# The first pass over eight experts: instructions written out in place of a loop on four engines

## The chip, the cores and the metric

The kernel runs on one core of a Trainium2 chip. The metric is the device time of one execution in microseconds. The kernel before takes 1589.56 us (median of three runs, 1588.62 to 1594.91).

## The reference

Two encoder layers on one sequence of 256 tokens of width 1024, all in float32. Layer 0 mixes tokens with dilated attention and a RWKV-7 scan and ends in a dense SwiGLU. Layer 1 mixes with a short convolution and a gated DeltaNet and ends in a mixture of experts, which is the part that matters here:

```python
def moe_swiglu(h, router, w_gate, w_up, w_down):
    probs = jax.nn.softmax((h @ router).astype(jnp.float32), axis=-1)
    top_p, top_i = lax.top_k(probs, TOP_K)                    # 2 of 8
    top_p = top_p / jnp.sum(top_p, axis=-1, keepdims=True)
    gates = einsum(top_p, one_hot(top_i, N_EXPERTS))
    out = jnp.zeros_like(h)
    for e in range(N_EXPERTS):                                # 8 experts, 1024 -> 3584 -> 1024
        out = out + gates[..., e:e+1] * swiglu(h, w_gate[e], w_up[e], w_down[e])
    return out
```

Each expert has three matrices of 1024 x 3584 floats. Every one of them is read once from HBM in a pass.

## The kernel before, in words

The five engines run five instruction streams, each written by hand in its own block and tied together by semaphores; no planner orders them. Up to the router (some 660 us) all streams are straight code. The expert stage follows.

A pass of the expert stage holds up to 96 tokens for every expert (three blocks of 32). If some expert was chosen by more than 96 tokens, a flag makes all engines run up to two further passes; otherwise the `If` at the end of each stream skips them. In a pass every expert is done in two halves of its 3584 hidden columns. A half, numbered n from 0 to 15, has three phases on TensorE: `project("gate")`, `project("up")` (both at line 3139, 192 matmul records) and `down` (line 3164, 336 records). That makes 48 phases. The function `phase` (line 569) gives their order: gate 0, up 0, gate 1, up 1, down 0, then gate n, up n, down n-1 for n from 2 on, and down 15 at the end.

Weights pass through one ring of eight units in SBUF, 896 KB each; one phase uses the whole ring. SyncE (`load_phase`, `load_unit`, line 618) waits for each unit until TensorE has released it in the phase before (`unit_ps`), then issues the DMA of the next phase's unit. TensorE waits for a unit's landing (`landed_e`) just before its first matmul on it. So a unit has one phase, less the time of its own use, to be issued, moved and landed.

ScalarE applies SiLU to the gate banks and scales an expert's result (`silu`, `result`). VectorE multiplies by the up banks and transposes (`hidden`), and computes the row numbers of the next expert's tokens. GpSimd gathers those rows from HBM and adds finished rows back by indirect DMAs; its stream has no loop in it.

Four streams write the middle of a pass as a hardware loop (`Fori`): SyncE with 7 turns of six phases (line 638), ScalarE with 6 turns (line 1297), VectorE with 6 turns (line 2188) and TensorE with 6 turns (line 3202). One TensorE turn is

```python
with pe.Fori(0, NE - 2) as i:
    project("gate", ps, i, 2); project("up", ps, i, 2); down(ps, i, 1)
    project("gate", ps, i, 3); next_rows(ps, i, 2)
    project("up", ps, i, 3);   turn_rows(ps, i, 2); down(ps, i, 2)
```

that is, phases 5 to 10 in the first turn, 11 to 16 in the second, and so on to phase 40. Before it phases 0 to 4 stand as straight code, behind it phases 41 to 47. Every semaphore target inside is an expression in i, such as `i * (6 * NU) + ...`, so in a loop it is a register's value, and the expert's number in a DMA source (`bass.ds(i + 1, 1)`) is one too.

Of the kernel before, what the change touches and what calls it, by code (L numbers as in the profile page):

```python
# [25 lines left out]
NE = 8  # L26
# [70 lines left out]
def hybrid_trunk(nc, A, out):  # L97
# [16 lines left out]
    with ctx:  # L114
# [446 lines left out]
        @block.sync  # L561
        def _(sp):
            def load(kind, n):
                s, prev, _ = where[kind, n]
                if prev:
                    sp.wait_ge(*used_up(*prev))
                v = ring[:, s * SLOT:(s + 1) * SLOT]
                v8 = v.rearrange("p (k n) -> p k n", k=KT)
                kt = "o (k p) n -> p (o k) n"
                if kind == "ev_in":  # L570
                    parts = [(v8, A["ev_w_in"][:, :, 512 * n:512 * n + 512].rearrange(kt, p=P))]
                elif kind == "lora1":
                    w = v[:, 0:KT * 384].rearrange("p (k n) -> p k n", k=KT)
                    parts = [(w[:, :, 64 * z:64 * z + 64], A["ev_w1"][:, z].rearrange(kt, p=P)) for z in range(2)]
                    parts += [(w[:, :, 128 + 64 * z:192 + 64 * z], A["ev_a1"][:, z].rearrange(kt, p=P)) for z in range(2)]
                    parts += [(w[:, :, 256:384], A["ev_g1"].rearrange(kt, p=P))]
                elif kind == "lora2":
                    parts = [(v[:, 0:512], A["ev_w2"].rearrange("o z r c -> (o z r) c")),
                             (v[:, 512:1024], A["ev_a2"].rearrange("o z r c -> (o z r) c")),
                             (v[:, 1024:1536], A["ev_g2"].rearrange("o r c -> (o r) c"))]  # L580
                elif kind in ("ev_out", "od_out"):
                    w = A["ev_w_out" if kind == "ev_out" else "od_w_out"]
                    parts = [(v8, w[:, :, 512 * n:512 * n + 512].rearrange(kt, p=P))]
                elif kind == "ffn_in":
                    parts = [(v8[:, :, 256 * i:256 * i + 256],
                              A[w][:, :, 256 * n:256 * n + 256].rearrange(kt, p=P))
                             for i, w in enumerate(("ev_ffn_gate", "ev_ffn_up"))]
                elif kind == "ffn_down":
                    k = min(4, FF // P - 4 * n)
                    parts = [(v[:, 0:k * D].rearrange("p (k n) -> p k n", k=k),  # L590
                              A["ev_ffn_down"][:, 512 * n:512 * n + k * P, :].rearrange(kt, p=P))]
                elif kind == "od_in":
                    parts = [(v8, A["od_w_in"][:, :, 512 * n:512 * n + 512].rearrange(kt, p=P))]
                for dst, src in parts:
                    if (kind, n) == ("ev_in", 0):
                        sp.dma_start(dst[:, 0:4, :], src[:, 0:4, :]).then_inc(w0_in, 16)
                        dst, src = dst[:, 4:8, :], src[:, 4:8, :]
                    sp.dma_start(dst, src).then_inc(landed[s], 16)

            for a in range(TT):  # L600
                sp.dma_start(x_sb[:, a, :], A["x"][0, P * a:P * a + P, :]).then_inc(x_in[a], 16)
            sp.dma_start(vecrows[0:N0, 0, :], A["vecs"][0:N0, :]).then_inc(vec_in, 16)
            sp.dma_start(vecrows[0:N1, 1, :], A["vecs"][N0:N0 + N1, :]).then_inc(vec_in, 16)
            load(*chunks[0][:2])
            load(*chunks[1][:2])
            sp.dma_start(pos_i[:, :], A["positions"].rearrange("b (a p) -> p (b a)", p=P),
                         allow_slow_non_contiguous=True).then_inc(small_in, 16)
            sp.dma_start(rows[:, :], A["rows"].to_broadcast([P, A["rows"].shape[1]])).then_inc(small_in, 16)
            sp.dma_start(wsmall[:, :], A["wsmall"]).then_inc(small_in, 16)
            for kind, n, _ in chunks[2:]:  # L610
                load(kind, n)
            if UPTO >= 4:
                packed_w = {"gate": A["od_moe_gate"], "up": A["od_moe_up"], "down": A["od_moe_down"]}

                def load_unit(kind, e, s, u):

                    src = packed_w[kind][e, NU * s + u].rearrange("o p n -> p (o n)")
                    sp.dma_start(ring[:, UNIT * u:UNIT * u + UNIT], src).then_inc(landed_e[u], 16)

                def load_phase(ps, i, kind, e, n):  # L620

                    f = phase(kind, n)
                    for u in range(NU):
                        if f or ps:
                            sp.wait_ge(unit_ps, units_used(ps, i, f - 1, u))
                        elif u < 7:
                            sp.wait_ge(*used_up(*before[-(-(UNIT * u + UNIT) // SLOT) - 1 if UNIT * u + UNIT <= NSTAT * SLOT
                                                       else NSTAT - 1]))
                        load_unit(kind, e, n % 2, u)

                def expert_pass(ps):

                    load_phase(ps, 0, "gate", slice(0, 1), 0)
                    load_phase(ps, 0, "up", slice(0, 1), 0)
                    load_phase(ps, 0, "gate", slice(0, 1), 1)
                    load_phase(ps, 0, "up", slice(0, 1), 1)
                    load_phase(ps, 0, "down", slice(0, 1), 0)
                    with sp.Fori(0, NE - 1) as i:
                        for n in (2, 3):
                            load_phase(ps, i, "gate", bass.ds(i + 1, 1), n)  # L640
                            load_phase(ps, i, "up", bass.ds(i + 1, 1), n)
                            load_phase(ps, i, "down", bass.ds(i + (n - 2), 1), n - 1)
                    load_phase(ps, 0, "down", slice(NE - 1, NE), 2 * NE - 1)

                def store(ps):

                    for q in range(4):
                        c = slice(512 * (q % 2), 512 * (q % 2) + 512)
                        sp.wait_ge(cmb_sb, 8 * ps + 2 * q + 2)
                        sp.dma_start(out[0, P * (q // 2):P * (q // 2) + P, c], x_sb[:, q // 2, c]).then_inc(stored, 16)  # L650

                expert_pass(0)
                store(0)
                sp.wait_ge(flag_rdy, 1)
                with sp.If(sp.value_load(flag[0:1, 0:1], min_val=0, max_val=1) > 0):
                    for ps in range(1, PASSES):
                        sp.wait_ge(stored, 64 * ps)
                        expert_pass(ps)
                        store(ps)
                    sp.wait_ge(stored, 64 * PASSES)  # L660
                sp.wait_ge(stored, 64)
# [149 lines left out]
        def _(act):  # L811
# [428 lines left out]
            if UPTO >= 4:  # L1240
# [52 lines left out]
                def all_experts(ps):  # L1293

                    silu(ps, 0, 0)
                    silu(ps, 0, 1)
                    with act.Fori(0, NE - 2) as i:
                        silu(ps, i, 2)
                        result(ps, i, 0)
                        silu(ps, i, 3)  # L1300
                    silu(ps, 0, 2 * NE - 2)
                    result(ps, 0, NE - 2)
                    silu(ps, 0, 2 * NE - 1)
# [15 lines left out]
        def _(dve):  # L1319
# [728 lines left out]
            if UPTO >= 4:  # L2048
# [128 lines left out]
                def all_experts(ps):  # L2177
# [7 lines left out]
                    next_rows(ps, 0, 1)  # L2185
                    hidden(ps, 0, 1)
                    weigh_tokens(ps, 0, 1)
                    with dve.Fori(0, NE - 2) as i:
                        select(bass.ds(i + 2, 1))
                        hidden(ps, i, 2)  # L2190
                        dve.wait_ge(rows_added, i * (16 * NB) + 16 * (ADDED * ps + TT + 1 + NB))
                        next_rows(ps, i, 2)
                        hidden(ps, i, 3)
                        weigh_tokens(ps, i, 2)
                    select_last(ps)
                    hidden(ps, 0, 2 * NE - 2)
                    hidden(ps, 0, 2 * NE - 1)
# [17 lines left out]
        def _(pe):  # L2215
# [855 lines left out]
            if UPTO >= 4:  # L3071
# [116 lines left out]
                def all_experts(ps):  # L3188
# [10 lines left out]
                    project("up", ps, 0, 1)  # L3199
                    turn_rows(ps, 0, 1)  # L3200
                    down(ps, 0, 0)
                    with pe.Fori(0, NE - 2) as i:
                        project("gate", ps, i, 2)
                        project("up", ps, i, 2)
                        down(ps, i, 1)
                        project("gate", ps, i, 3)
                        next_rows(ps, i, 2)
                        project("up", ps, i, 3)
                        turn_rows(ps, i, 2)
                        down(ps, i, 2)  # L3210
                    last_n = 2 * NE - 2
                    project("gate", ps, 0, last_n)
                    project("up", ps, 0, last_n)
# [53 lines left out]
```

## Time and profile before

| | us |
|---|---|
| median of three runs | 1589.56 |
| the profiled execution | 1595.33 |
| its span, first to last instruction | 1593.6 |
| expert stage, first matmul of phase 0 to the last of phase 47 | 659.96 to 1583.19 |
| mean granted clock of TensorE (1.00 is 2.4 GHz) | 0.98 |

The engine rows of a profile count an instruction as busy from its start to its end, and matmuls overlap, so a busy TensorE need not be at its peak. The chain of waits is followed backwards from the last instruction; "issue" in it is time in which an engine waited for nothing that the profile shows. The column PEclk is the clock granted to TensorE as a share of 2.4 GHz, and the DMA share is the mean busy share of the 16 DMA engines; it can pass 1.00 a little where packets overlap.

### The profile page before, as it was taken

To read this page: it belongs to the slowest core of one execution; us is meant where nothing else is said; L and a number is where in the kernel's file an instruction comes from. 1 tells how busy PE (TensorE), PEld (TensorE's weight loads), DVE (VectorE), ACT (ScalarE), POOL (GpSimd) and SP (SyncE) were. 2 spreads that over 40 slices of the span, in tenths; PEclk is the share of its full clock that TensorE was granted. 3 is DMA by queue.
4 is the path that set the end of the run, shared out by engine and by line. 5 is a ranking of instruction groups with operands and counts; after the bars stand their busy time and mean duration, and the time that the engine had idled before them with its cause. 6 is when DMAs were issued, how large, how long until landed. Compare 5 with 4: busy or idle time off the path is not lost.

```text
span 1593.6 us, 35986 instructions
## 1 busy us (share of the span) xinstructions
PE 1547.3 (97%) x16151; PEld 942.2 (59%) x16151; DVE 491.4 (31%) x897; ACT 329.6 (21%) x560; POOL 104.0 (7%) x145
## 2 busy tenths in 40 slices
PE   9999999999999999999998998998998998999998
PEld 5868886999989976534343444444444444444435
DVE  5888465655456683311001001001001001001000
ACT  5455333543358432200000000000000000000000
POOL 3004000000000010010010010010010010010000
PEclk9999799999999999999999998999999999999999
DMA  7510013555553410899999998998998998999995
GB/s 259 149 46 26 1 54 106 185 186 197 173 185 107 149 63 1 305 419 417 418 405 372 392 395 357 377 397 361 387 399 354 388 402 352 390 401 419 405 407 240
DMA packets 111360, 440.09 MB, mean 276 GB/s; under 512 B 12330, under 2 KB 38846, under 8 KB 111198
## 3 DMA queue, kind: packets, MB, share of 16 engines
q1 hardware_dynamic: 106014, 427.90, 68.9%
q0 software_dynamic: 5184, 9.70, 2.2%
q8 instruction: 142, 2.33, 0.6%
q14 instruction: 20, 0.16, 0.0%
HBM read 430.62 MB, written 6.95 MB: 275 GB/s over the span
## 4 chain that ended last, share of the span: by engine, by line
PE 92%; DVE 4%; issue 2%; ACT 1%; DMA 0%; SPq 0%; DVEq 0%
PE bank L3139 37%; PE bank L3164 18%; PE bank L2297 5%; PE bank L2298 5%; PE bank L2296 5%; PE bank L3021 2%; PE bank L2263 2%; PE bank L2726 2%; PE bank L2316 1%; PE bank L2277 1%; PE bank L2393 1%; PE bank L2329 1%; ACT ehf L1207 1%; PE bank L2518 1%; PE bank L2610 1%
## 5 line engine op out<-in xcount | busy, mean ns | idle before, releaser
L3139 PE MATMUL bank<-ring,arena 128*32 128x448 f32 x6144 | 597.5, 546 | 29.1 <-issue 28.4
L3139 PEld LDWEIGHTS bank<-ring,arena 128*32 128x32 f32 x6144 | 216.7, 111 | 394.7 <-issue 393.1
L3164 PE MATMUL bank<-ring,arena 128*32 128x256 f32 x5376 | 295.0, 379 | 0.0
L3164 PEld LDWEIGHTS bank<-ring,arena 128*32 128x32 f32 x5376 | 177.5, 110 | 115.6 <-issue 4.6
L2161 DVE TENSOR_TENSOR arena<-bank,arena 128x448 f32<-128x448 f32 x48 | 28.7, 598 | 572.6 <-PE bank L3139 572.6
L1282 ACT ACTIVATE arena<-bank 128x448 f32<-128x448 f32 x48 | 26.1, 543 | 594.8 <-PE bank L3139 594.8
L2297 PE MATMUL bank<-ringr,split 128*128 128x256 f32 (+1 forms) x488 | 146.9, 301 | 0.0
L2296 PE MATMUL bank<-ehr_,split 128*128 128x256 f32 x400 | 113.3, 283 | 0.0
L2298 PE MATMUL bank<-ehr_,ringr 128*128 128x256 f32 x400 | 111.9, 280 | 0.0
L1772 DVE TENSOR_TENSOR ringr<-ring,split 128x2048 fp32r<-128x2048 f32 x33 | 75.5, 2291 | 72.8 <-ACT split L1090 72.8
L2297 PEld LDWEIGHTS bank<-ringr,split 128*128 128x128 f32 x488 | 91.7, 188 | 4.0 <-issue 0.2
L782 POOL DMA_INDIRECT xsum<-arena,row_now x21 | 33.4, 1590 | 664.8 <-ACT arena L1290 660.6
L1090 ACT ACTIVATE split<-ring 128x2048 fp32r<-128x2048 f32 x33 | 63.0, 1912 | 63.2 <-DMA ring<-in_ev_ffn_up 31.7
L2298 PEld LDWEIGHTS bank<-ehr_,ringr 128*128 128x128 f32 x400 | 76.0, 190 | 0.0
L2296 PEld LDWEIGHTS bank<-ehr_,split 128*128 128x128 f32 x400 | 75.1, 188 | 0.4 <-issue 0.2
L2141 DVE COPY row_now<-row_next 128x3 int32<-128x3 int32 x7 | 1.2, 169 | 223.9 <-PE bank L3104 223.9
L1290 ACT ACTIVATE arena<-bank,small 128x256 f32<-128x256 f32 x21 | 8.4, 471 | 246.5 <-PE bank L3164 246.5
L2296 PE MATMUL bank<-split 128*128 128x512 f32 (+1 forms) x120 | 43.7, 364 | 0.0
L2857 PE MATMUL bank<-scr,ring 128*128 128x256 f32 x160 | 38.3, 388 | 0.3 <-issue 0.3
L2298 PE MATMUL bank<-split 128*128 128x512 f32 x88 | 34.6, 393 | 0.0
L2298 PE MATMUL bank<-split,ringr 128*128 128x256 f32 x112 | 31.5, 282 | 0.0
L2163 DVE STREAM_TRANSPOSE arena<-arena 128x448 f32<-128x448 f32 x48 | 31.0, 645 | 1.7
(566 smaller groups left out, 1591.7 us busy)
## 6 DMA issues: line engine op xcount, KB each, us to landing
ring<-in_od_moe_gate SPq DMA_DIRECT2D x128, 896.0 KB, 8.0
ring<-in_od_moe_up SPq DMA_DIRECT2D x128, 896.0 KB, 9.0
ring<-in_od_moe_down SPq DMA_DIRECT2D x128, 896.0 KB, 10.0
ring<-in_od_w_in SPq DMA_DIRECT2D x7, 2048.0 KB, 7.7
ring<-in_ev_ffn_gate SPq DMA_DIRECT2D x11, 1024.0 KB, 5.5
ring<-in_ev_ffn_up SPq DMA_DIRECT2D x11, 1024.0 KB, 8.0
ring<-in_ev_w_in SPq DMA_DIRECT2D x5, 2048.0 KB, 9.0
ring<-in_ev_ffn_down SPq DMA_DIRECT2D x5, 2048.0 KB, 7.7
```

The source lines that it names most:

```text
L782: pool.indirect_dma_start(xsum, bass.IndirectOffsetOnAxis(row_now[:, b:b + 1], 0), ysb[:, b, :], None, compute_op=ADD).then_inc(rows_added ...
L1090: act.activation(homes[q % NHOME], ring[:, v], ACT.Copy).then_inc(pc_hi, 1)
L1772: dve.tensor_tensor(ringr[:, v], ring[:, v], homes[q % NHOME].bitcast(F32), SUB).then_inc(pc_lo, 1)
L2263: last = pe.matmul(B[bank][:, :], h[:, k, P * a:P * a + P], w8[:, k, :], start=(k == 0), stop=(k == KT - 1))
L2296: pe.matmul(o, sh, mh, start=start, stop=False, skip_group_check=True)
L2297: pe.matmul(o, sh, ml, start=False, stop=False, skip_group_check=True)
L2298: return pe.matmul(o, sl, mh, start=False, stop=stop, skip_group_check=True)
L2726: last = pe.matmul(B[2 * n + a][:, :], yT[:, k, P * a:P * a + P], w8[:, k, :], start=(k == 0), stop=(k == KT - 1))
L2857: last = pe.matmul(B[t % 2][:, SEQ * f:SEQ * f + SEQ], w8[:, k, c:c + P], hT[:, k, :], start=(k == 0), stop=(k == KT - 1))
L3021: last = pe.matmul(B[2 * n + a][:, :], yTo[:, k, P * a:P * a + P], w8[:, k, :], start=(k == 0), stop=(k == KT - 1))
L3139: last = pe.matmul(bank[BT * g:BT * g + BT, 0:FC], xg[:, k % 2, P * b + BT * (k // 2):P * b + BT * (k // 2) + BT], ring[:, UNIT * k + FC * ...
L3164: last = pe.matmul(B[6 + b // 2][BT * g:BT * g + BT, DC * (b % 2):DC * (b % 2) + DC], hdT[:, n % 2, b, BT * kk:BT * kk + BT], pieces_of(q) ...
```

## The change

On SyncE, ScalarE, VectorE and TensorE the loop's body becomes a function `expert(i)`. In the first pass (`ps == 0`) a Python loop calls it with i = 0, 1, 2, ..., so that the instructions of every turn stand one behind the other, with constants in place of register values. The further passes keep the hardware loop. TensorE's part, and SyncE's:

```diff
-                    with pe.Fori(0, NE - 2) as i:
+                    def expert(i):
                         project("gate", ps, i, 2)
                         project("up", ps, i, 2)
                         down(ps, i, 1)
...
+                    if ps == 0:
+                        for i in range(NE - 2):
+                            expert(i)
+                    else:
+                        with pe.Fori(0, NE - 2) as i:
+                            expert(i)
```

```diff
-                    with sp.Fori(0, NE - 1) as i:
+                    def expert(i):
                         for n in (2, 3):
                             load_phase(ps, i, "gate", bass.ds(i + 1, 1), n)
...
+                    if ps == 0:
+                        for i in range(NE - 1):
+                            expert(i)
+                    else:
+                        with sp.Fori(0, NE - 1) as i:
+                            expert(i)
```

ScalarE and VectorE have the same edit around their loops of NE - 2 turns. GpSimd's stream is as before. No operation, wait or buffer is added, removed or moved in order.

## Rows read from the trace of the kernel before

**Rows 1.** The page, part 4: the chain that ended last, by engine.

```profile
PE 92%; DVE 4%; issue 2%; ACT 1%; DMA 0%; SPq 0%; DVEq 0%
```

**Rows 2.** The page, part 2: granted TensorE clock in 40 slices of 39.84 us.

```profile
PEclk9999799999999999999999998999999999999999
```

**Rows 3.** Costliest groups by line: records; busy us, mean ns; idle before, releaser.

```profile
L3139 PE MATMUL bank<-ring,arena 128*32 128x448 f32 x6144 | 597.5, 546 | 29.1 <-issue 28.4 <-DVE arena L2152 0.7
L3164 PE MATMUL bank<-ring,arena 128*32 128x256 f32 x5376 | 295.0, 379 | 0.0
```

**Rows 4.** The chain in order of time, 752 to 995: start us, us, what.

```profile
752.76 36.08 PE bank L3139 x384
...
844.53 18.27 PE bank L3164 x336
862.80 5.14 issue
867.94 3.94 PE bank L3139 x17
871.88 1.51 issue
873.38 34.40 PE bank L3139 x364
...
982.12 3.94 issue
```

**Rows 5.** TensorE's waits, 863 to 1456: releaser, us, times, longest.

```profile
PE bank L3139 <- issue: 28.4, 10, 5.1
```

**Rows 6.** Stretches: length, busy us (records) per engine, clock, DMA share, GB/s.

```profile
752.57:862.80 110.23, 110.23 (x1454) 47.44 (x1446) 8.99 (x21) 4.46 (x9) 7.68 (x6) 1.00 1.02 413
862.80:982.12 119.32, 112.68 (x1450) 51.87 (x1450) 8.99 (x21) 4.46 (x9) 7.70 (x6) 0.97 0.98 386
1101.60:1219.50 117.90, 112.84 (x1451) 50.90 (x1450) 8.99 (x21) 4.46 (x9) 7.71 (x6) 0.97 0.97 382
1337.88:1456.09 118.21, 112.50 (x1454) 52.21 (x1458) 9.69 (x24) 4.46 (x9) 7.71 (x6) 0.99 0.97 381
1456.09:1566.30 110.21, 110.21 (x1466) 47.85 (x1462) 7.16 (x12) 5.33 (x11) 5.97 (x5) 1.00 1.02 409
...
879.50:982.12 102.62, 102.62 (x1373) 48.34 (x1365) 8.99 (x21) 4.46 (x9) 7.70 (x6) 1.00 1.01 400
```

**Rows 7.** The same view around one turn's end.

```profile
862.00:868.00 6.00, 0.86 (x20) 0.29 (x16) 0.00 (x0) 0.00 (x0) 0.00 (x0) 0.77 1.01 413
868.00:874.00 6.00, 4.49 (x25) 1.19 (x29) 0.00 (x0) 0.00 (x0) 0.00 (x0) 0.66 0.60 245
```

**Rows 8.** Ring loads, to landing, at 700:753, 753:863, 880:982, 1456:1566 in that order.

```profile
DMA to landing us min/median/max: 10.5/13.4/14.5
DMA to landing us min/median/max: 10.5/12.2/14.1
DMA to landing us min/median/max: 6.0/7.5/10.8
DMA to landing us min/median/max: 7.0/8.7/12.1
```

**Rows 9.** DMA of 752.57 to 862.80: all packets; queue, packets, MB, share.

```profile
DMA packets 7585, 45.56 MB, mean 413 GB/s; under 512 B 875, under 2 KB 1259, under 8 KB 7570
q8 instruction: 12, 0.20, 0.7%
```

**Rows 10.** The same queue of 862.80 to 982.12.

```profile
q8 instruction: 14, 0.23, 0.7%
```

**Rows 11.** Waits of ScalarE and VectorE in the expert stage.

```profile
ACT arena L1282 <- PE bank L3139: 594.8, 48, 63.2
DVE arena L2161 <- PE bank L3139: 572.6, 16, 59.5
```

**Rows 12.** SyncE's queue in order of time, 835 to 880.

```profile
847.49 15.84 SPq L618 DMA_DIRECT2D ring<-in_od_moe_gate  x8
```

More of the change, by code:

```diff
@@ L1296, in all_experts @@
                     silu(ps, 0, 1)
-                    with act.Fori(0, NE - 2) as i:
+                    def expert(i):
                         silu(ps, i, 2)
@@ L1300, in all_experts @@
                         silu(ps, i, 3)
+                    if ps == 0:
+                        for i in range(NE - 2):
+                            expert(i)
+                    else:
+                        with act.Fori(0, NE - 2) as i:
+                            expert(i)
                     silu(ps, 0, 2 * NE - 2)
@@ L2187, in all_experts, with expert @@
                     weigh_tokens(ps, 0, 1)
-                    with dve.Fori(0, NE - 2) as i:
+                    def expert(i):
                         select(bass.ds(i + 2, 1))
@@ L2194, in all_experts @@
                         weigh_tokens(ps, i, 2)
+                    if ps == 0:
+                        for i in range(NE - 2):
+                            expert(i)
+                    else:
+                        with dve.Fori(0, NE - 2) as i:
+                            expert(i)
                     select_last(ps)
@@ L3201, in all_experts, with expert @@
                     down(ps, 0, 0)
-                    with pe.Fori(0, NE - 2) as i:
+                    def expert(i):
                         project("gate", ps, i, 2)
@@ L3210, in all_experts @@
                         down(ps, i, 2)
+                    if ps == 0:
+                        for i in range(NE - 2):
+                            expert(i)
+                    else:
+                        with pe.Fori(0, NE - 2) as i:
+                            expert(i)
                     last_n = 2 * NE - 2
```

## The prediction

> **What bounds the kernel now.** I read the chain that ended last first: TensorE holds 92% of it, and 2% is "issue", time that nothing in the profile explains [rows 1]. The grouped lines put that time in one place: the expert projections of line 3139 have 28.4 us of it in front of them, the down projections of line 3164 none [rows 3]. The record counts also say that only the first pass runs: 6144 is 32 projections of 192, and 5376 is 16 downs of 336. The further passes, which keep their loop, are skipped, so the edit covers all that is executed.
>
> Then the chain in order of time, to see where the 28.4 us stand. From 752.76 to 862.80, the loop's first turn, matmuls follow each other without a hole. Then come 5.14 us of nothing, 17 matmuls in 3.94 us, 1.51 us of nothing, and full pace again; at 982.12 it starts over [rows 4]. There are ten such holes in five pairs [rows 5], one pair for each of the loop's five jumps back. None stands at the entry of the loop (752.57) or at its exit (1456.09). I conclude that the cost is the jump: behind a taken branch TensorE has no instructions. The hole is not a semaphore, for it has no releaser and its place is the first instructions of the body.
>
> The third view prices a whole turn. The first turn, entered from above, takes 110.23 us; the second 119.32, the fourth 117.90, the last 118.21; the straight code behind the loop, with nearly the same work in it, 110.21 [rows 6]. The holes are only part of the 8 to 9 us: in the stretches around one the granted clock is 0.77 and 0.66 in place of 1.00 [rows 7], a mixture of 2.4 and 1.2 GHz, after TensorE had stood still. The clock by slices of 40 us almost hides that: it has one 8 in the whole expert stage [rows 2], so a short fall has to be looked for at the hole itself. Hence 17 matmuls in 3.94 us, 232 ns each, where 384 in 36.08 us are 94 ns each [rows 4].
>
> **The change, part by part.** *TensorE's jumps.* Five turns run from 862.80 to 1456.09, which is 593.29 us; five turns at the first one's 110.23 us are 551.15. The difference is 42.1 us: 28.4 holes [rows 5] and 13.7 slow clock behind them. Written out, each turn is entered as the first one was, from the instruction above it. I take all 42.1 away. A larger gain I exclude: the first turn already had the loop's register arithmetic in it and went at the pace of straight code, so that constants in place of registers save nothing on the path.
>
> *Instructions fetched.* The instruction queue brought 12 packets, 0.20 MB, in the first turn and 14, 0.23 MB, in the second [rows 9, 10]. So a turn is fetched anew each time in the loop too, and written out it is fetched no more often. Price: nothing, and a gain of at most 0.03 MB a turn. Its cover is that fetching runs ahead in straight code; what it would cost without that is the third rival.
>
> *The other three engines.* ScalarE and VectorE waited 594.8 and 572.6 us for TensorE's projections [rows 11]; their jumps lie in such waits, gone or not. SyncE's turn ends before phase 11's first load, which was issued at 847.49 [rows 12]. TensorE could release that unit after 48 of the 336 records of phase 10, that is at 844.53 + 48/336 x 18.27 = 847.1 [rows 4]: no delay from SyncE's jump is seen. All three: nothing. If one did show through, it would be a gain of at most a hole such as TensorE's, 5 us, five or six times over, but no wait of TensorE for them stands in the trace.
>
> *What is late next: the weights.* This is the only cost I can see. The 5 us at each jump also gave the DMAs time; the share fell to 0.60 behind the hole [rows 7]. Without it they must keep TensorE's pace from start to end. The room: a phase lasts 18.1 us and uses a unit for an eighth, 2.3, so that a load has 15.9 us from release to need. After a jump loads take 7.5 us (at most 10.8). Where no jump comes for long, they take 13.4 (14.5) before the loop, 12.2 (14.1) in the first turn, and 8.7 (12.1) behind the loop [rows 8]. So the queue grows by about 1 us a turn where it is short and shrinks by 1 where it is long. I expect it to settle near 12, under 15.9, as in the first turn, which ran with no wait for a landing at 413 GB/s. Bounds: nothing (the first turn), and, if 400 GB/s, the lowest rate of a stretch of 100 us at full share [rows 6], were all the DMAs can do: 45.56 MB [rows 9] then take 113.9 us a turn, 3.7 more, over 6.15 turns' worth to the end 22.6 us. I take 1.5 us, near the first turn, which is the nearest row: the same work, the same full queue.
>
> Sum for the profiled execution: 1595.33 - 42.1 + 1.5 = 1554.7 us. The median of the runs is 5.8 us lower. If those 5.8 us lie outside the jumps, the median becomes 1589.56 - 40.6 = 1549.0; if they lie in jumps that cost less in the other runs, it stays at 1554.7. The turns themselves differ by 1.4 us [rows 6], so part of it may. I take 1551.
>
> **Two rules against it.** The trace's jump costs 42.1/5 = 8.4 us. The Trainium skill (Advanced Engine Details and Errata, Control Flow Timing) gives about 51 ns for a branch and 108 for a compare-and-branch; an estimate by it is 5 x 0.16 = 0.8 us for all five, and the sum would be 1589. The holes disagree, unless they have another cause; that is the second rival. The trace moves 413 GB/s in the first turn. The Trainium skill (DMA: Bandwidth & Descriptors, Where 436 GB/s comes from) holds that some 358 GB/s bind a transfer from HBM to SBUF; an estimate by it is 45.56 MB in 127 us a turn, more than today's 118, and no gain at all. The trace, with 413, contradicts it here.
>
> **The rivals.**
> 1. *The DMAs take half back.* The queue keeps growing by 1 us a turn past 15.9, and TensorE waits in small pieces inside a phase, at the 400 GB/s bound: 1589.56 - 42.1 + 22.6 = 1570; the stretch between my forecast and there is this case's. For it: DMA share 1.01 to 1.02 wherever no jump is near. Against it: the shrinking queue of the first turn.
> 2. *The hole is not the jump's.* The body's head waits for something that the profile doesn't record, or the DMAs need the pause: the time stays 1589. For it: "issue" is only the absence of a recorded releaser. Against it: the first turn has the same head and no hole.
> 3. *Slower: straight code starves TensorE of instructions.* The place is the down phases, which use instructions fastest: 672 records (matmuls and their weight loads) in 18.27 us, so a packet of 16 KB, 256 instructions (0.23 MB in 14 packets), lasts 7.0 us. A packet fetched at a jump took up to 5.14 us. With loads that take 12.2 in place of 7.5 us a fetch could take 5.14 x 12.2/7.5 = 8.4 us and be 1.4 late. There are some 2.6 packets in each of 13 downs left after phase 10, 34 in all: 47 us lost, 5 more than is won, about 1595. It is slower from 8.2 us a fetch on. Against it: phases 7 and 10 ran with a long queue and no hole.
>
> **How the numbers follow.** Forecast, 1544 to 1557: 0.80. Rival 1, 1557 to 1575: 0.13. Rival 2, within 0.5% (8 us, about what a measurement here can tell from no change): 0.04. Rival 3: 0.03. So faster 0.93, same 0.04, slower 0.03. The range reaches from a little under the full 42.1 us off the fastest run, 1544, to the 400 GB/s bound, 1570.
>
> **What would show it.** Right: no "issue" in front of line 3139 after phase 10, a clock of 1.00 through the expert stage, turns of 110 to 111 us, loads that take 11 to 14 us, the span near 1553. Wrong in the DMA step: waits of TensorE for landings in short pieces, most in the phases in which rows are gathered and added back, and turns of 112 to 114. Wrong in the main step: holes at the same places, at 862.80 and then every 118 us, or new ones in the down phases.

## The result, and the profile after

The changed kernel takes 1542.72 us (median of four runs, 1540.90 to 1543.81) beside 1592.24 us for the kernel before (four runs, 1588.62 to 1602.31). The ratio is 0.968, 95% interval 0.963 to 0.973. It is faster, as forecast, but by 49.5 us where 40.6 were summed up, and 1.3 us below the forecast range. A second comparison, with six runs of it and eleven of the kernel before, gave 0.972 (0.967 to 0.977).

The page of the changed kernel: the chain by engine, the clock by slices, and the two groups that answer to [rows 1 to 3].

```profile
PEclk9999999999999999999999999999999999999999
...
PE 93%; DVE 4%; ACT 1%; issue 1%; DMA 0%; SPq 0%; DVEq 0%
...
L3160 PE MATMUL bank<-ring,arena 128*32 128x448 f32 x6144 | 581.7, 539 | 0.7 <-DVE arena L2166 0.7
...
L3185 PE MATMUL bank<-ring,arena 128*32 128x256 f32 x5376 | 293.0, 379 | 0.0
```

The 28.4 us of "issue" in front of the projections are gone, and so is the slow clock behind them: a projection's mean is 539 ns, where it was 546. The chain of the changed kernel in order of time answers to [rows 4]; the first line is the start of the expert stage:

```profile
648.96 18.25 PE bank L3160 x192
...
741.75 36.08 PE bank L3160 x384
...
833.52 18.27 PE bank L3185 x336
851.79 36.08 PE bank L3160 x384
...
943.56 18.27 PE bank L3185 x336
```

Down 10 (833.52) runs straight into gate 11 (851.79), where 5.14 + 1.51 us of nothing stood. The stretches of the changed kernel answer to [rows 6], with the first turn and the fourth; the upper two lines are a stretch long before the experts.

```profile
153.00:165.00 12.00, 11.32 (x157) 9.89 (x160) 7.37 (x17) 3.80 (x10) 1.16 (x1) 1.00 0.01 3
165.00:180.00 15.00, 14.65 (x157) 13.56 (x158) 9.99 (x18) 6.70 (x16) 2.49 (x2) 1.00 0.01 2
741.75:851.79 110.04, 110.04 (x1454) 47.75 (x1450) 9.09 (x21) 4.46 (x9) 7.68 (x6) 1.00 1.02 413
1071.87:1181.91 110.04, 110.04 (x1454) 47.75 (x1450) 8.99 (x21) 4.46 (x9) 7.71 (x6) 1.00 1.02 409
```

And the same two early stretches of the kernel before:

```profile
153.00:165.00 12.00, 11.51 (x117) 8.34 (x116) 5.62 (x12) 3.03 (x8) 1.73 (x1) 0.59 0.00 1
165.00:180.00 15.00, 15.00 (x83) 14.77 (x82) 4.69 (x10) 1.53 (x4) 0.00 (x0) 0.53 0.00 1
```

Here is the part that I had not forecast. In the profiled execution before, the clock was at its lower level, 1.2 GHz, from 155.2 to 179.1 us (and for 3.4 us from 138.2); in the one after it was not. The expert stage starts at 648.96 where it started at 659.96. So the spans' 54.7 us (1593.6 less 1538.9) are 11.0 ahead of the experts, 43.1 in the expert stage (923.23 less 880.13), and 0.6 behind it.

Loads of the ring in the changed kernel, from issue to landing, in turns one, four and six, answer to [rows 8]:

```profile
DMA to landing us min/median/max: 10.5/12.2/13.7
DMA to landing us min/median/max: 9.8/11.8/14.4
DMA to landing us min/median/max: 9.7/11.6/13.2
```

They settle near 12, under the 15.9 us of room, and TensorE waits for no landing.

### The profile page after: what moved, and what is told of

It reads as the page before. It is cut to its first block, busy times and chain, and to the rows that moved or that the text cites. A ratio compares the mean times of both kernels' runs of the same rounds, so it can differ in the third digit from the quotient of the medians.

```text
span 1538.9 us, 34875 instructions
## 1 busy us (share of the span) xinstructions
PE 1518.5 (99%) x16138; PEld 913.3 (59%) x16151; DVE 491.1 (32%) x897; ACT 329.7 (21%) x560; POOL 104.7 (7%) x145
## 4 chain that ended last, share of the span: by engine, by line
PE 93%; DVE 4%; ACT 1%; issue 1%; DMA 0%; SPq 0%; DVEq 0%
PE bank L3160 38%; PE bank L3185 19%; PE bank L2318 5%; PE bank L2319 5%; PE bank L2317 5%; PE bank L3042 2%; PE bank L2284 2%; PE bank L2747 2%; PE bank L2337 1%; PE bank L2298 1%; PE bank L2350 1%; ACT ehf L1214 1%; PE bank L2539 1%; PE bank L2878 1%; PE bank L2564 1%
## 5 line engine op out<-in xcount | busy, mean ns | idle before, releaser
L3160 PE MATMUL bank<-ring,arena 128*32 128x448 f32 x6144 | 581.7, 539 | 0.7 <-DVE arena L2166 0.7
L3160 PEld LDWEIGHTS bank<-ring,arena 128*32 128x32 f32 x6144 | 200.0, 110 | 368.5 <-issue 365.2
L3185 PEld LDWEIGHTS bank<-ring,arena 128*32 128x32 f32 x5376 | 173.9, 110 | 117.6 <-issue 4.8
L759 POOL TENSOR_TENSOR arena<-arena,levmask 128x512 f32<-128x512 f32 x4 | 7.5, 1904 | 363.8 <-DVE xn L1629 349.1
## 6 DMA issues: line engine op xcount, KB each, us to landing
ring<-in_od_moe_up SPq DMA_DIRECT2D x128, 896.0 KB, 12.2
```

The costliest lines, as they stand in the source:

```text
L3160: last = pe.matmul(bank[BT * g:BT * g + BT, 0:FC], xg[:, k % 2, P * b + BT * (k // 2):P * b + BT * (k // 2) + BT], ring[:, UNIT * k + FC * ...
L3185: last = pe.matmul(B[6 + b // 2][BT * g:BT * g + BT, DC * (b % 2):DC * (b % 2) + DC], hdT[:, n % 2, b, BT * kk:BT * kk + BT], pieces_of(q) ...
```

## The experiments

Theory A: only TensorE's far jumps (jumps back over a whole turn) cost, each two holes and a slow clock; the rest of the gain is the early slow clock, which has nothing to do with the change. Its rivals are named in the expectations.

**e1, the kernel before again** (no edit).

> The kernel before, unchanged, to see what its time is made of in other executions. Theory A (the jumps account for 43 us in every execution, the rest of the gain was a slow clock early in the profiled execution before, 155 to 179 us, that comes by chance): a ratio of 1.00, five pairs of holes again, the expert stage from its first to its last matmul at 921 to 925 us, and the early stretch at clock 1.00 in some executions, so that the first expert matmul starts between 649 and 660 us. Rival B (the written-out code itself shortened the stage ahead of the experts, for instance by another placement of its instructions): the first expert matmul starts at 659 to 661 us again, with the same slow clock at 155 to 179 us.

Median 1589.3, ratio 0.997 (0.994 to 1.001); ten runs from 1583.62 to 1597.31. Its profile has no slow clock at 153 to 180 us, and its expert stage starts at 651.11: rival B falls. It has another fall of the clock a little earlier, at 137 us, worth some 2 us against 648.96:

```profile
138.00:145.00 7.00, 7.00 (x33) 5.93 (x34) 6.86 (x8) 2.16 (x4) 3.95 (x2) 0.50 0.01 2
...
153.00:165.00 12.00, 11.90 (x163) 10.10 (x163) 5.08 (x12) 5.18 (x14) 2.50 (x2) 1.00 0.01 1
```

Its five turns take 598.2 us (853.94 to 1452.12 in the chain), 48.0 more than five of 110.04; in the first profile of the kernel before it was 43.1. So my figure for the expert stage held only roughly: the jumps' price differs between executions by 5 us. Of that, 1.2 us are in the holes (29.6 us in sum, where they were 28.4); the rest goes with how long the clock stays low: in the five turns it was at its lower level for 44.4 us here and for 30.7 us in the first profile.

**e2, TensorE alone written out, and e3, the other three alone.** Each takes the edit of the one side:

```diff
 # e2: SyncE, ScalarE, VectorE keep their Fori        # e3: TensorE keeps it
+                    if ps == 0:
+                        for i in range(NE - 2):
+                            expert(i)
```

> TensorE's turns written out; SyncE, ScalarE and VectorE keep their loops. Theory A (only TensorE's jumps lie on the path): the whole gain, 1540 to 1545 us, turns of 110.0 us without a hole. Rival C (SyncE's jump delays the loads, or VectorE's and ScalarE's jumps delay a bank): a loss of up to 5 us for each of 5 or 6 jumps comes back, 1550 to 1570 us, with waits of TensorE for landings or banks at the turns' ends.

> SyncE, ScalarE and VectorE written out; TensorE keeps its loop. Theory A: no gain, 1585 to 1595 us, the same five pairs of holes, turns of 118 to 119.5 us. Rival C: 5 to 30 us of gain. Rival B (the placement of code ahead of the experts): the start of the expert stage moves as much as in the changed kernel.

e3: 1593.91 us, ratio 1.000 (0.997 to 1.004), and its five turns have 43.4 us too many; no part of the gain is theirs that these runs could tell from nothing. Its ten holes stand in TensorE's waits as before:

```profile
PE bank L3160 <- issue: 27.8, 10, 5.1
```

e2: 0.973 (0.967 to 0.978), but its four runs are 1541.35, 1552.63, 1553.42 and 1553.65, above my 1545. Its turns are the changed kernel's, 110.03 us (863.60 to 973.63 in the chain), with no hole and no wait for a load, so rival C falls. The 11 to 12 us are the early clock again (the expert stage of the profiled execution starts at 660.76), now with no far jump on TensorE ahead of it or in the expert stage; the stretch of e2:

```profile
153.00:165.00 12.00, 11.96 (x114) 8.81 (x115) 4.92 (x11) 3.03 (x8) 1.02 (x1) 0.52 0.00 1
```

Why the others' jumps are free is in the branch instructions of the kernel before, which were not among my rows (line, engine's queue, count, min/median/max ns):

```profile
L3202 PEldq COMPARE_BRANCH  x6: 83/5542/6086, 861.4 to 1454.7; - x6
...
L638 SPq COMPARE_BRANCH  x7: 40/45/50, 844.2 to 1546.9; - x7
...
L2188 DVEq COMPARE_BRANCH  x6: 50/56/72, 845.6 to 1438.9; - x6
...
L1297 ACTq COMPARE_BRANCH  x6: 40/45/45, 825.2 to 1418.5; - x6
```

The hole on TensorE is the branch itself: 83 ns where the loop ends, 4.9 to 6.1 us where it jumps back over some 2,900 instructions. On the other three engines, whose bodies are short (26 records a turn in the trace on ScalarE, 44 on VectorE, 170 on SyncE), the loop's branch takes 40 to 72 ns.

**e4, two experts a turn**, three turns, two jumps:

```diff
+                        with pe.Fori(0, (NE - 2) // 2) as j:
+                            expert(j * 2)
+                            expert(j * 2 + 1)
```

> TensorE loops three times over two experts in place of six times over one, so that two jumps are left of five; the other engines are written out. Theory A (a fixed price per jump): 3/5 of 43 us is saved on TensorE, two pairs of holes, 8.6 us each, about 17 us above the changed kernel: 1558 to 1563 us. Rival D (the price grows with the length of the body, since more must be fetched anew): nearly all of the loss stays, 1575 to 1590 us.

1571.3 us (1570.22 to 1572.70), ratio 0.987 (0.982 to 0.991), 8 us above the range. The profile has a slow clock at 154 us, and its expert stage starts at 661.09: these are the 11 to 12 us that the forecast left out. One of its two jumps, in the chain:

```profile
973.97 5.10 issue
979.07 3.94 PE bank L3160 x17
983.00 1.64 issue
...
1093.38 36.08 PE bank L3160 x384
```

The expert behind it takes 119.4 us, the one behind the other jump 118.9: 9.1 us a jump on the mean. A body twice as long costs little more, if anything (8.6 to 9.6 us in the three profiles of the shorter one); rival D falls.

**e5, a near jump**, and **e10, longer and longer near jumps**: a loop of two turns ahead of five experts.

```diff
+                            if i:
+                                with pe.Fori(0, 2):
+                                    for _ in range(4):     # e10: (30, 60, 120, 240, 480)[i - 1]
+                                        pe.matmul(B[7][:, 384:512], ident[:, :], ident[:, :], ...)
                             expert(i)
```

> The changed kernel with a hardware loop of two turns on TensorE in front of five of the six experts; its body is four matmuls of 128x128 into columns that nothing reads, so that each of the five places has one jump back to an instruction a few places before it. Theory A in its narrower form (the hole is the fetching of a far target's instructions): holes under 1 us, the clock stays at 1.00, and each place costs its 8 matmuls, 16 records of about 0.12 us each or 2 us, plus at most 1: turns of 112 to 113 us. Rival E (every taken jump drops what was fetched ahead and fetches anew, however near the target): holes of 4 to 5 us and a clock fall at each place, turns of 118 to 121 us.

> Where a jump begins to cost: the changed kernel with five two-turn loops on TensorE as before, with bodies of 30, 60, 120, 240 and 480 unread matmuls (four instructions each: 120, 240, 480, 960 and 1920 instructions; a turn of the experts has some 2,900). If only a target that is no longer held costs a fetch: no hole (under 0.3 us) at the small ones, and 4 to 6 us with a clock fall from some size on, the same from there. If the price grows with the distance: a hole that rises step by step. If any body over 256 instructions, one block of the instruction queue, costs: holes at 480, 960 and 1920. The matmuls themselves add 2 x 930 x 0.25 = 465 us.

e5, one of the five places in its chain:

```profile
862.14 1.98 PE bank L3238 x16
864.13 36.22 PE bank L3160 x384
```

and e5's branches:

```profile
L3236 PEldq COMPARE_BRANCH  x10: 76/144/240, 861.2 to 1310.8; - x10
```

Every place costs its matmuls and at most some tenths of a us; a near jump takes at most 0.24 us, and no hole shows while it lasts. (The single time, 1562.29 us, has the early slow clock in it.) Rival E falls. In e10 the bodies of 120 to 960 instructions show no hole; the one of 1920 shows one:

```profile
1506.22 107.39 PE bank L3238 x960
1613.62 1.33 issue
1614.95 1.16 PE bank L3238 x8
```

Its branch took 3.3 us, and the clock did not fall. So the cost starts between 960 and 1920 instructions, in one execution and with one jump of each size; neither the 4 to 6 us nor the clock fall that I expected from there on came. Why 1920 costs less than 2,900 was not tested by itself, but the traces point at the weights' loads: here they had stopped (2 GB/s from 1600 to 1613.6 us), while they moved 413 GB/s at the jump of the kernel before [rows 7]. The branch behind the experts that skips the further passes, with the loads at rest too, takes 3.9 us in the kernel before and 3.4 in the changed one.

**e6, more bytes**, two more ring units loaded per expert:

```diff
...
+                                sp.dma_start(scr[:, 0:UNIT], packed_w["up"][slice(i, i + 1), n]...).then_inc(w0_in, 16)
```

> The changed kernel with two more ring units of 896 KB loaded per expert into memory that nothing reads, 50 in place of 48 per turn. A measure of the step in which I feared the loads. If the DMAs give no more than the 413 GB/s of the first turn before: 45.05 + 1.84 MB take 113.5 us a turn, 3.5 above 110.04, TensorE waits in short pieces, and the time is about 20 us above the changed kernel's. If they have more to give: turns of 110 us, landings of 12 to 15 us, no change in time.

1572.42 us, 30 above the changed kernel where I expected about 20, and TensorE's waits are loads now:

```profile
PE bank L3168 <- DMA ring<-in_od_moe_gate: 14.8, 30, 1.4
PE bank L3168 <- DMA ring<-in_od_moe_up: 2.6, 5, 1.0
...
PE bank L3193 <- DMA ring<-in_od_moe_down: 0.4, 1, 0.4
```

The expert stage is 909.5 us (651.22 to 1560.74), 29.4 more. The 14 added units are 12.8 MB, 31.2 us at the 412 GB/s that this run moved at full share. By that estimate the changed kernel has some 2 us to spare in its whole expert stage: the loads hide, but only just.

**e7, the changed kernel again** (no edit), and **e8, with ten more early matmuls** that nothing reads; **e9, the loops kept, with the same ten.**

```diff
+                if p == 0 and lev == LEV0 and g:
+                    for _ in range(4):
+                        unread_level(B[2 + g])
                 pe.wait_ge(x_cp, inv_seq(p, lev, g))
...
                     elif q < 2 or i >= 4:
                         pe.wait_ge(sc_sb, n - 2)
+                        if q < 2:
+                            unread_level(B[SC_BANK[q][i % 4]])
```

> The changed kernel again, for its own spread. Theory A (the slow clock at about 154 us comes by chance, whatever stands behind it): part of the executions at 1552 to 1555 us and part at 1540 to 1544, as with the kernel in which TensorE alone was written out. Rival B (the change itself took the early slow clock away): all at 1540 to 1544.

> The changed kernel with ten more matmuls that nothing reads (128x512 in bf16, some 0.2 to 0.4 us each) on TensorE at 138 to 153 us, ahead of the place where the clock fell: four in a hole of 0.8 us, six between the scores. If the sparse work there brings the fall and this fills enough of it: all executions at 1540 to 1545 us. If not: two groups again, 11 to 12 us apart, both up to 2 us later.

> The kernel before, all loops in place, with the same ten unread matmuls at 138 to 153 us. Theory A with the early slow clock as a second, separate term: its upper group (1592 to 1603 us, two thirds of the executions of the kernel before) disappears, all executions at 1584 to 1590, 42 to 48 us above the written-out kernel with the same matmuls, and the ratio to the kernel before is 0.993 to 0.996. Rival: two groups again as in the kernel before; then the one group of the written-out kernel with these matmuls was chance.

e7: four runs at 1541.26 to 1543.41 and two at 1559.69 and 1560.01, with mean clocks of 0.986 in place of 0.996 to 0.999. A slow clock comes in executions of the changed kernel too, so rival B falls; that its first four had none that costs 11 us was luck. Neither of the two long ones was profiled, and they stand above my 1552 to 1555: that their clock fell at the same place is not shown, and why they lost 17 us and not 11 stays open. e8: six runs from 1542.71 to 1546.39, one of them 1.4 us above my range, no upper group; ratio 0.969 (0.966 to 0.972).

e9 missed my range: 1598.44 us (twelve runs, 1594.71 to 1601.66), ratio 1.003 (1.001 to 1.005). There is no early slow clock in its profile (1.00 at 153 to 165 us; the experts start at 649.51), but its jumps cost more. Its chain:

```profile
852.35 5.07 issue
857.42 1.72 PE bank L3144 x8
859.14 3.77 issue
862.91 37.00 PE bank L3144 x376
...
973.88 4.65 issue
```

The second hole comes behind 8 matmuls, not 17, and is longer. The five turns have 52.7 us too many (852.35 to 1455.29). All that e9 adds to the kernel before is 20 instructions, executed at 138 to 153 us, which moved the loop's head on by as much.

**e11, the loop's head moved on**, e9 with 24 more instructions at the start of the stream:

```diff
-            unread_start(6)
+            unread_start(12)
```

> The kernel with all loops and the ten early matmuls, with six more unread matmuls (24 instructions) at the start of TensorE's stream, up to 3 us there, so that the loop's head moves by 24 instructions. In the kernel before, the second hole of a turn came behind 17 matmuls, and in the one with the ten matmuls (20 instructions further on) behind 8, both about 11.9 us after the jump. Theory F (the second hole is the fetch of the next block of 256 instructions, and the head lay about 40, then 20 instructions ahead of a block's end): now the head lies just behind a block's start, the second hole disappears, a jump costs its first hole of 4 to 5.2 us and 2 to 4 us of slow clock, turns of 116 to 119 us, against 120.5 on the mean with the ten matmuls alone: 1582 to 1590 us. Rival G (the second hole is a wait for something else, such as a load): it stays, behind 8 to 17 matmuls, and turns stay at 118 to 122 us.

1577.74 us (1575.78 to 1579.53), ratio 0.991 (0.987 to 0.995), 20.7 us below e9. Its chain:

```profile
854.05 5.13 issue
859.18 37.62 PE bank L3144 x384
...
970.75 4.36 issue
```

The second hole is gone in all five turns, as theory F says; they have 32.6 us too many (854.05 to 1436.85), 6.5 a jump, less than I expected, and the time is 4 us below my range. Rival G falls. So the first hole is the wait for the block in which the target lies, and the second that for the next block, when the target lies near the first one's end. The traces hold the blocks themselves, as packets of 16 KB on the instruction queue. In the kernel before, at 864.9 to 866.2 and at 870.7 to 871.9 us:

```profile
q8 instruction: 1, 0.02, 5.2%
...
q8 instruction: 1, 0.02, 5.6%
```

The first of the two runs from 865.02 to 866.09, and the branch that began at 861.44 ends at 867.52; the second runs from 870.78 to 871.85, and the matmuls go on at 873.38. In every far jump of the kernel before, e1, e3, e4, e9 and e11 the branch ends 1.4 to 1.6 us behind a packet's end. That packet starts 2.4 to 3.7 us after the branch while the weights stream, and 0.9 us after it in e10's far jump, beside loads at rest.

## Why the prediction was right in sign and short in size

*The main step was right in mechanism.* "Behind a taken branch TensorE has no instructions": shown by the branch records, by e2 against e3, by e5, by e11 and by the instruction packets. The Trainium skill (Runtime: NRT & Kernel Launch, Instruction fetch mechanics) has the same: instructions arrive in blocks of 256, fetched ahead in order, and a taken branch to a target outside the two blocks held waits for a fetch. The trace agrees that a far jump waits, with branches of 4.9 to 6.1 us; on TensorE more than two blocks can be jumped back over, since 960 instructions cost no hole. The branch times that I weighed against the change (the Trainium skill, Advanced Engine Details and Errata, Control Flow Timing) are of the size of the near jumps in e5 (0.08 to 0.24 us) and fail for the far one.

*Its size was a little short.* I measured the straight turn from 752.57 and got 110.23; the chain's own piece starts at 752.76, and a straight turn is 110.04. Five times 0.19 is the missing 1.0 us: in that execution the jumps cost 43.1, not 42.1.

*The loads* cost nothing, where I took 1.5 us. The row I chose, the first turn, was the right one, for they settled at 11.6 to 12.2. e6 shows that the fear of rival 1 was not idle: 4% more bytes and TensorE waits.

*The step that failed* is the sum: "1595.33 - 42.1 + 1.5 = 1554.7", which came out at 1540.90. It put everything outside the jumps at no change. Of the 13.8 us, 11.0 are the slow clock ahead of the experts, almost all of it at 155 to 179 us, which stood in the execution I subtracted from. A row of mine showed it, the slice with a 7 [rows 2], and I read that row for the expert stage alone and let the 7 stay as if it belonged to the kernel. It comes and goes: this fall is in the profiles of the kernel before, e2, e4, e5 and e10, and not in those of the changed kernel, e1, e3, e6, e7, e8, e9 and e11. The remaining 2.8 are the 1.0 and 1.5 above and 0.3 at the ends.

*The range's lower end* failed with it. I took a fixed 42.1 off the fastest run, 1588.62, and little more. But the jumps themselves cost 43.1 to 48.0 us in three profiles of the loop at that place (the kernel before, e1, e3). The median went from 1589.56 to 1542.72, 46.8 us, where I had 40.6 off. The run of 1589.56 was not profiled, so what it lost by jumps and what by an early slow clock stays open; jumps of that price alone would put it at 1541.6 to 1546.5. The median of the kernel before was 1589 to 1597 in later sets, whose runs lie from 1582 to 1603; by the profiles the early slow clock is a part of that spread. The 5.8 us between profile and median, which I split, fit that clock better than cheap jumps in the median's run: the jumps of the profiled execution were the cheapest of the three. The prediction also names two upper ends, 1557 in its chances and 1570 in the sentence behind them; the first is its range.

*SyncE, ScalarE, VectorE* at nothing: right (e3). *Instructions fetched* at nothing: right, with 129 packets on the instruction queue in the whole execution where there were 142. *Rival 3*, straight code that starves, did not come: the down phases ran without a hole. It had mis-sized a step too: it took the hole of 5.14 us for the fetch of one packet, but in the traces of both kernels' expert stages a packet takes 0.9 to 1.1 us from start to end, and the rest of a far branch lies ahead of the packet's start and behind its end.

What stays open is why the clock falls at 153 to 155 us in some executions and not in others with the same instructions at nearly the same times. TensorE had been busy 13.1 to 14.3 of the 15 us before, with small matmuls and a hole of 0.5 to 0.8 us; in the profile of the changed kernel, which has no fall, it was 13.2 and 0.8. Another fall, at 137 to 138 us, comes and goes as well: it lasts 10.2 us in the profiles of e1, e6 and e7, none of which has the later one, and 3.4 us in those of the kernel before, e5 and e11. With the ten matmuls, no profile of three (e8, e9, e11) has the later fall and no run of 24 stands 11 us off its group; that they prevent it is likely and not proven, since the fall also stays away without them, and e11 has the earlier one in spite of them.

Of the versions tried, the changed kernel with the ten matmuls (e8) has the same median as the changed kernel beside it, 1543.37 both, and the smaller spread in six runs each, 3.7 us against 18.8.

## What to carry to other kernels

A hardware loop on TensorE with a body of some 2,900 instructions paid a fetch at each jump back, and about half as much again in slow clock; write such a loop out where it lies on the path, and leave short ones alone (up to 960 instructions cost no hole here). Look at the duration of its branch instructions first: they show the price directly. Where a loop must stay, the place of its head counts: 24 instructions moved were worth 20 us in five turns. Before a sum is taken off a profiled execution, look for a slow clock anywhere in it, also where nothing is changed, and ask whether the other runs have it.

## What the runs showed of the hardware

A jump back over 960 instructions cost no hole on TensorE, over 1920, with the loads at rest, one of 1.33 us, over some 2,900 a first hole of 3.9 to 5.2 us and, by the head's place, a second of up to 3.8. The second block does not wait for the matmuls: its packet starts 4.3 to 5.8 us after the first one's in the kernel before and in e9, and the matmuls went on 8.6 to 10.6 us after the first hole began in both, 9.5 and 9.4 on the mean, whether 17 or 8 of them had filled the time. In each first hole, or just behind it, the clock fell to its lower level and stayed there for 3.4 to 10.2 us, which the windows before showed as 0.66 to 0.77 [rows 7]; with one hole only (e11) the first gate and up phases took 37.6 us (39.1 in one turn) in place of 36.08.
